# A hybrid attention, pooling, mLSTM and expert layer: finer expert searches, later gating, twelve gate blocks moved into the first pass's branches, and another order of the first loads

## The reference

```
def _layer(x, is_prompt, st, p, rel_bias):
    xn = _rmsnorm(x, p['norm1_g'])
    z = xn @ p['w_in']
    aq, ak, av, pin, cq, ck, cv, ci, cf, co, ga, gb, gc = jnp.split(z, _split_points(), axis=-1)
    ...
    merged = (jax.nn.sigmoid(ga) * (ya @ p['w_br_a']) + jax.nn.sigmoid(gb) * (yb @ p['w_br_b'])
              + jax.nn.sigmoid(gc) * (yc @ p['w_br_c']))
    x = x + merged @ p['w_out']
    x = x + _peer(_rmsnorm(x, p['norm2_g']), ...)

def _peer(x, wq, k1, k2, u, v):     # per block of tokens
    q = (xb @ wq).reshape(blk, PEER_HEADS, 2, PEER_DK // 2)
    s1 = jnp.einsum('thd,kd->thk', q[:, :, 0], k1);  s2 = jnp.einsum('thd,kd->thk', q[:, :, 1], k2)
    v1, i1 = lax.top_k(s1, 16);  v2, i2 = lax.top_k(s2, 16)
    cand = v1[..., :, None] + v2[..., None, :]       # 256 pairs, the best 16 are the experts
    gates = softmax(top_v)
    act = gelu(einsum('td,thkd->thk', xb, u[experts]))
    y = einsum('thk,thkd->td', gates * act, v[experts])
```

## Time and profile before

| | us |
|---|---|
| median of three runs | 3745.59 |
| lowest, highest | 3741.58, 3746.2 |
| the profiled execution | 3749.68 |
| its span in the trace | 3747.9 |
| first gather issued, from the span's start | 395.3 |
| first pass: first matmul of project, branches, merge, output, find | 19.5, 122.3, 193.4, 321.4, 366.2 |
| second pass: the same | 540.2, 712.2, 835.9, 1072.4, 1139.5 |
| third pass: the same | 1335.7, 1527.9, 1659.3, 1895.7, 1963.5 |
| last pass: the same | 2164.2, 2363.5, 2672.1, 2890.0, 2967.1 |

### The profile page before, as it was taken

The page is one execution under the profiler, slowest core; times in us unless marked ns, Lnnn a source line. Parts: engine busy times, 40 slices in busy tenths (PEclk is TensorE's granted clock), DMA queues, the critical chain, the costliest instruction groups (busy, mean ns, idle before and its releaser), DMA issues. The chain is left out here.

```text
span 3747.9 us, 31564 instructions
## 1 busy us (share of the span) xinstructions
PE 3148.9 (84%) x10006; PEld 1809.0 (48%) x10006; DVE 2254.2 (60%) x5201; ACT 1102.6 (29%) x3314; POOL 1174.5 (31%) x1038
## 2 busy tenths in 40 slices
PE   7798879979988889889979799873699898777777
PEld 4587644446665444446655444431466563332222
DVE  1411767674556768865557779872455487764544
ACT  1210333342223333432223324441111233332222
POOL 0000333333333333433323233331233234444442
PEclk9899989989998999999989899986899999999999
DMA  5134889989999999999999899984899699999998
GB/s 168 64 134 158 348 364 387 359 321 365 420 419 361 400 368 414 404 366 391 420 385 392 351 390 402 379 331 175 320 382 397 254 402 404 421 421 421 422 421 356
DMA packets 204912, 1317.39 MB, mean 352 GB/s; under 512 B 23234, under 2 KB 27386, under 8 KB 72097
## 3 DMA queue, kind: packets, MB, share of 16 engines
q0 software_dynamic: 148608, 1082.20, 71.4%
q1 hardware_dynamic: 52681, 220.59, 15.8%
q10 hardware_dynamic: 3456, 12.58, 0.9%
HBM read 1298.97 MB, written 17.64 MB: 351 GB/s over the span
## 5 line engine op out<-in xcount | busy, mean ns | idle before, releaser
L1862 POOL DMA_INDIRECT arena<-uv,eidx x1032 | 1173.9, 1138 | 2544.9 <-PE ps L889 1812.5
L889 PE MATMUL ps<-arena,dgs 128*128 128x512 f32 x3412 | 1638.2, 624 | 310.2 <-ACT dgs L1190 286.4
L1432 DVE CUSTOM_DVE_ANT_0 arena<-arena,xx 128x1024 f32<-128x1024 f32 x1024 | 1232.9, 1222 | 513.1 <-DMA arena<-uv,eidx 488.6
L889 PEld LDWEIGHTS ps<-arena,dgs 128*128 128x128 f32 x3412 | 651.5, 198 | 1122.0 <-issue 669.0
L1171 ACT ACTIVATE gel<-dots 128x2 f32<-128x2 f32 x516 | 104.3, 202 | 1524.7 <-DVE dots L1432 1524.0
L922 PE MATMUL ps<-wbuf,xT 128*128 128x420 f32 (+1 forms) x1152 | 426.1, 519 | 10.2 <-DMA wbuf<-w_z 9.1
L1070 PE MATMUL ps<-xT,wbuf 128*128 128x256 f32 (+1 forms) x1536 | 358.1, 387 | 7.9 <-DMA wbuf<-w_merge 5.8
L1070 PEld LDWEIGHTS ps<-xT,wbuf 128*128 128x128 f32 x1536 | 295.4, 193 | 78.3 <-issue 18.6
L922 PEld LDWEIGHTS ps<-wbuf,xT 128*128 128x128 f32 (+1 forms) x1152 | 204.2, 180 | 232.6 <-issue 220.6
L1190 ACT ACTIVATE dgs<-cst,wgt 128x128 f32<-128x128 f32 x853 | 305.3, 395 | 16.7
L1667 DVE SCALAR_TENSOR_TENSOR T<-T,ps 128x256 f32<-128x256 f32 (+1 forms) x96 | 40.6, 423 | 429.7 <-PE ps L1074 429.7
(11 more groups left out here) (352 smaller groups left out, 1871.5 us busy)
## 6 DMA issues: line engine op xcount, KB each, us to landing
wbuf<-w_merge SPq DMA_DIRECT2D x96, 768.0 KB, 8.5
wbuf<-w_z SPq DMA_DIRECT2D x64, 840.0 KB, 8.7
wbuf<-w_q SPq DMA_DIRECT2D x64, 512.0 KB, 8.1
arena<-uv,eidx POOLq DMA_INDIRECT x1032, 11.6
wbuf<-w_o SPq DMA_DIRECT2D x32, 512.0 KB, 7.4
xin<-x_prompt SPq DMA_DIRECT2D x8, 1024.0 KB, 8.3
grow<-gains SPq DMA_DIRECT2D x8, 512.0 KB, 8.5
xin<-biasfull SPq DMA_DIRECT2D x4, 1024.0 KB, 5.0
```

The lines of the kernel that those rows point to most:

```text
L889: done = mm(ps[:, half, :], dgs[:, j, :], ring[:, j, row_], start=(q == 0), stop=(q == P - 1), skip_group_check=True)
L1432: v.tensor_tensor_reduce(ring[:, j, 0:D], ring[:, j, 0:D], x, 1.0, 0.0, ALU.mult, ALU.add, dots[:, j:j + 1]).then_inc(s["dotted"], 1)
L1862: g.indirect_dma_start(ring[:, j, :], None, uv, bass.IndirectOffsetOnAxis(ap=experts, axis=0)).then_inc(got[j], 16)
```

## The change

It has five parts. The number of slots per stage and `KEPT` stay.

1. **First loads.** SyncE loads x, `cst`, the gains and two `w_z` blocks; the six smaller tables follow (`load_tables`) before the third `w_z` block. The bucket product goes behind the first weight block on TensorE (`buckets`), its copy behind the norm on VectorE. `spread_bias` is issued by ScalarE, behind the copies of the first pair of blocks. TensorE waits for the transposed x of one tile at a time.
2. **Twelve gate blocks.** In the first pass, the gate products of merge units 0 to 11 are computed inside the branches, at five places of each tile (`EARLY_AT`: 1, 2, 1, 1, 0 and 1, 2, 1, 1, 2 blocks), in PSUM banks 0 and 1, and ScalarE copies them to a place that the ring uses later. Two thirds of their `w_merge` blocks are loaded for it, and the last third in the merge.
3. **Later gating.** VectorE's gate of unit k-1 comes between the points of unit k. ScalarE's tanh comes behind the first point of its unit, not ahead of it.
4. **Finer searches.** `topk` has eight places for slots and not four, and in `find` TensorE and ScalarE have a point ahead of each of the two query blocks, and two at the similarities. In `project` each place takes one tile's point.
5. **Slots on VectorE.** `ON_VECTOR` gives it a second place of the eight in `project` (the last pass has four already), a fourth in the last pass's merge, and a fourth in `output`: 197 slots of 1032, and before it was 171. By stage: second pass's project 6 to 12, third pass's 7 to 15, last merge 23 to 31, the three outputs 5, 5, 3 to 6, 6, 5.

The diff, cut to its core:

```diff
+EARLY = 12
+EARLY_AT = ({3: 1, 5: 2, 6: 1, 8: 1, 9: 0}, {3: 1, 5: 2, 6: 1, 8: 1, 9: 2})
...
-    first = [(("f", h, i), 1 if h > 1 else 0) for h in range(PH) for i in range(2)]
-    search = [(("f", h, i), 52 / 16) for h in range(PH) for i in range(2)]
+    first = [(("f", h, i), 1 if h > 1 else 0) for h in range(PH) for i in range(4)]
+    search = [(("f", h, i), 52 / 32) for h in range(PH) for i in range(4)]
...
-ON_VECTOR = {"z": (3,), (LAST, "z"): (1, 3, 5, 7), "b": (1, 5), "m": (1, 4, 6), "o": (1, 3, 5), "f": (2,)}
+ON_VECTOR = {"z": (3, 7), (LAST, "z"): (1, 3, 5, 7), "b": (1, 5), "m": (1, 4, 6), (LAST, "m"): (1, 3, 5, 7), "o": (1, 3, 5, 7), "f": (2,)}
...
+        early = arena[:, NT * ZW + 2048:NT * ZW + 2048 + EARLY * TOK].rearrange("p (u n) -> p u n", u=EARLY)
...
+        def unit(p, i):
+
+            return p * UNITS + i + (EARLY if p or i >= NZ else 0)
...
-            sp.dma_start(cst[:, :], consts[:, 0:C_KEEP]).then_inc(s["setup"], 16)
-            sp.dma_start(T[:, 0:512], consts[:, C_KEEP:C_ALL]).then_inc(s["setup"], 16)
-            sp.dma_start(row[:, :], at(rows, 0, [[0, P], [1, R_ALL]])).then_inc(s["setup"], 16)
-            sp.dma_start(col[:, :], cols).then_inc(s["setup"], 16)
-            sp.dma_start(keys[:, :, :], keysT).then_inc(s["setup"], 16)
-            sp.dma_start(wpool[:, :, :], w_pool).then_inc(s["setup"], 16)
-            sp.wait_ge(s["init_v"], 1)
-            sp.dma_start(T[0:32, 512:520], rel).then_inc(s["setup"], 16)
...
+            sp.dma_start(cst[:, :], consts[:, 0:C_KEEP]).then_inc(s["consts_in"], 16)
+
+            def load_tables():
+
+                sp.wait_ge(s["init_v"], 1)
+                sp.dma_start(T[0:32, 512:520], rel).then_inc(s["setup"], 16)
+                sp.dma_start(T[:, 0:512], consts[:, C_KEEP:C_ALL]).then_inc(s["setup"], 16)
+                sp.dma_start(row[:, :], at(rows, 0, [[0, P], [1, R_ALL]])).then_inc(s["setup"], 16)
+                sp.dma_start(col[:, :], cols).then_inc(s["setup"], 16)
+                sp.dma_start(keys[:, :, :], keysT).then_inc(s["setup"], 16)
+                sp.dma_start(wpool[:, :, :], w_pool).then_inc(s["setup"], 16)
 
...
+            def weights(src, shape, count, sem, base, per, between=(), later=None, part=lambda i: (0, 1)):
...
+                    lo, hi = (int(width * x) for x in part(i))
+                    sp.dma_start(wbuf[:, k, lo:hi], src[i][:, lo:hi]).then_inc(w_in[k], 16)
...
-                weights(w_z, (HALF, ZP), NZ, s["z_mm"], NZ * tiles_before(p), tiles, [lambda: load_bias(p)] if p else [spread_bias], None if p else lambda: load_bias(p))
+                weights(w_z, (HALF, ZP), NZ, s["z_mm"], NZ * tiles_before(p), tiles, [lambda: load_bias(p)] if p else [load_tables], None if p else lambda: load_bias(p))
+                if p == 0:
+                    weights(w_merge, (12, P), EARLY, s["gate_mm"], 0, 1, part=lambda i: (0, 2 / 3))
...
+                        part=lambda i: (2 / 3 if p == 0 and i < EARLY else 0, 1))
...
+                if which:
+                    pe.wait_ge(s["xT_ready"], norms(p, which, len(tiles_of(p))))
...
+                        if c == 0:
+                            pe.wait_ge(s["xT_ready"], norms(p, 0, i + 1))
...
+                    if p == c == 0:
+                        buckets()
+
+            gates_done = [0]
+
+            def gates_early(units):
+
+                for u in range(gates_done[0], gates_done[0] + units):
+                    pe.wait_ge(w_in[u % 2], 16 * ((NZ + u) // 2 + 1))
+                    if u >= 2:
+                        pe.wait_ge(s["early_out"], u - 1)
+                    wv = wbuf[:, u % 2, 0:KC * P].rearrange("p (c n) -> p c n", c=KC)
+                    for c in range(KC):
+                        last = mm(ps[:, u % 2, 0:TOK], wv[:, c, :], xT[:, c, 0:TOK], start=(c == 0), stop=(c == KC - 1))
+                    last.then_inc(s["gate_mm"], 1)
+                gates_done[0] += units
 
...
+                    if p == 0:
+                        gates_early(EARLY_AT[t][3])
...
-                    for c in range(KC):
-                        last = mm(ps[:, 2 + 2 * b, m], wv[:, c, :], xT[:, c, m], start=(c == 0), stop=(c == KC - 1))
-                    last.then_inc(s["gate_mm"], 1)
+                    if p or k >= EARLY:
+                        for c in range(KC):
+                            last = mm(ps[:, 2 + 2 * b, m], wv[:, c, :], xT[:, c, m], start=(c == 0), stop=(c == KC - 1))
+                        last.then_inc(s["gate_mm"], 1)
...
+                    for k in range(2):
+                        point(p, "f", h, k)
+                        if h + 1 < PH:
+                            queries(h + 1, [k])
+                    point(p, "f", h, 2)
                     if h + 1 < PH:
                         similarities(h + 1)
+                    point(p, "f", h, 3)
...
+            def spread_bias():
+
+                act.wait_ge(s["buck_sb"], 1)
+                table = T[0:AH, 1024:1408]
+                act.dma_start(bass.AP(tensor=biasfull.tensor, offset=0, ap=[[2 * P, AH], [AH * 2 * P, P], [1, 2 * P]]),
+                              bass.AP(tensor=table.tensor, offset=table.offset + P - 1, ap=[table.ap[0], [-1, P], [1, 2 * P]])
+                              ).then_inc(s["scratch_w"], 16)
+
...
+                    if p == 0 and c == 1:
+                        spread_bias()
...
+            def gates_early(units):
+                for u in range(gates_kept[0], gates_kept[0] + units):
+                    act.wait_ge(s["gate_mm"], u + 1)
+                    f(early[:, u, :], ps[:, u % 2, 0:TOK], ACT.Copy).then_inc(s["early_out"], 1)
+                gates_kept[0] += units
...
-                    act.wait_ge(s["gate_mm"], 3 * KC * p + k + 1)
+                    point(p, "m", k, 0)
                     act.wait_ge(s["merged"], KC * p + k // 3 + 1)
-                    f(sgs[:, b, m], ps[:, 2 + 2 * b, m], ACT.Tanh, scale=0.5).then_inc(s["sig_done"], 1)
-                    point(p, "m", k, 0)
+                    if p == 0 and k < EARLY:
+                        act.wait_ge(s["early_out"], k + 1)
+                        f(sgs[:, b, m], early[:, k, :], ACT.Tanh, scale=0.5).then_inc(s["sig_done"], 1)
+                    else:
+                        act.wait_ge(s["gate_mm"], 3 * KC * p + k + 1)
+                        f(sgs[:, b, m], ps[:, 2 + 2 * b, m], ACT.Tanh, scale=0.5).then_inc(s["sig_done"], 1)
...
-                for k in range(3 * KC):
+
+                def gate(k):
                     b = k % 3
                     n = 3 * KC * p + k
-                    point(p, "m", k, 0)
                     dve.wait_ge(s["sig_done"], n + 1)
...
+                for k in range(3 * KC):
+                    point(p, "m", k, 0)
+                    if k:
+                        gate(k - 1)
                     point(p, "m", k, 1)
+                gate(3 * KC - 1)
...
+                between(0)
                 for k, t in pairs:
                     last = v.max_index(ii[:, k, t, 0:8], vv[:, k, t, 0:8], side_in[0:rows_, k, t, :])
                 last.then_inc(s["idx1"], 1)
-                if between:
-                    between(0)
+                between(1)
...
+                    search(p - 1, h, lambda i: at(4 * (h - SOON[p - 1]) + i // 2, i % 2))
...
-                    search(p, h, lambda i: point(p, "f", 2 * h + i // 2, i % 2))
+                    search(p, h, lambda i: point(p, "f", 2 * h + i // 4, i % 4))
...
```

119 lines of the change are left out of this document (66 added, 53 removed).

## The result

The changed kernel takes 3684.32 us (median of 4, 3682.12 to 3687.32) where the kernel before took 3745.89 beside it (median of 4): a ratio of 0.9835, 95% interval 0.9818 to 0.9852. That is 62 us less. The profiled execution took 3687.3 us (span 3685.5). The forecast was 3685. The total is met, and the sum behind it is not: the first pass gave half of what was forecast, the later passes half as much again. The rest of this document is about these two errors, which cancel; that they do is luck.

The account below looks back on a forecast made before the run. From 395 us on gather DMA bounds the kernel (377 GB/s against 420, 343 us shortfall); before, the first pass's own work. 3749.7 - 11.6 (opening) - 17 (gates) - 32 (later passes) = 3689.1, as median 3685 us; range 3655 to 3720.

Parts of the forecast that it names:

- Opening: First pass up to its branches: earlier norm and projection start and no weight-block wait save 11.6 us, bounds 2 and 14.
- With 4.5 us it is there; I take the whole 8.3: First projection: the fourth weight block, issued about 28, lands before 33.4 us, so TensorE's whole 8.29 us wait goes.
- Rival (3): First projection: the spread still delays a weight block, the fourth stalls, 10 us come back, 3695 us; chance 0.08.
- Twelve gates: First pass: gate blocks moved into branches cost 16 us there and save 33 in the merge, 17 us net.
- The walk through one tile: First pass's branches: five gate blocks of 17.25 us, partly filling TensorE's waits, make the first tile end 7 us later.
- Slots on VectorE: Later passes: moved slots save 7 us in the second projection, 1 in the third, 8 in last merge, 2 in outputs.
- Later gating: Merges of later passes: VectorE's gate after the next unit's dots saves 3 us in each of two merges.
- Finer searches: Find stages: eight points per search instead of four save 2.5 us in each of three, 0.5 in the first.
- (1) *Only the first pass pays: Later passes: already full where it matters, earlier freed slots only wait in the queue; 3717 us, chance 0.17.
- (5) *A slot on VectorE holds the ring longer: Later passes: 26 moved slots make GpSimd wait longer for VectorE, 95 us against 29 gained; 3811 us, chance 0.04.
- (4): First pass's branches: gates cost all of their 41.4 us and later passes give nothing; 3742 us, no change; chance 0.03.
- (2) *Nearly all: Later passes: they give nearly all they have, 65 us; 3652 us, chance 0.13.

Follow-up runs that it names:

- the three placings of the runs: Bias spread issued by ScalarE at 27.96 us (changed kernel, 0.9835), by SyncE at the same moment (0.9864), or by ScalarE near 9.5 us (0.9826).
- the run with that entry alone: Changed kernel without only the last merge's entry in VectorE's slot table (slots 1, 4, 6 of eight there, not 1, 3, 5, 7): ratio 0.9836 to the kernel before.

## Why the prediction was right, and where it was not

**Opening: forecast 11.6 us, measured -0.2.** The step that failed is "With 4.5 us it is there; I take the whole 8.3". The first half of the term held (start 14.33 instead of 13.8, bucket product with its copy 22.01 - 20.39 = 1.6 instead of 2.3 us). The prediction then followed the fourth block, issued at 28 and needed at 33.4, found it in time, and it was. It did not follow the fifth, issued at 33.6 with the spread in full course. With a spread of some 22 us and a load every 5.7, at least one load falls under it, wherever it stands; the three placings of the runs stall 12.21, 15.83 and 10.93 us. Loads that were issued while it ran took 10 to 18 us in the kernel before and in the changed one, where they take 4.5 alone. The row that said so stood in the earlier trace rows (a load of 13.9 us); I put it down to the place in the queue. Rival (3) is what happened, at a chance of 0.08, with 12.2 us for its 10, and on the next block. By the Trainium skill, DMA: Bandwidth & Descriptors, section Issuing engines are not separate DMA queues, a second issuer saves only the time of issuing, so the move to ScalarE's queue gives next to nothing; the runs agree to within 3.6 us (12.21 against 15.83). The same page, in the section Why a DMA increments its semaphore by 16 and not by 1, says that a DMA runs on the largest number of engines, 16 at most, that divides the slowest dimension of both of its sides, which is 8 here; the four or five tenths of the DMA view agree with it, and so do the 53.6% of the spread from DRAM. The 1.4 us for the half clock didn't come either, since a wait was still there: the clock was 0.50, its lower level of 1.2 GHz, from 46 to 52 us, and TensorE had been idle since 39.2:

```profile
46.00:52.00 6.00, 0.59 (x1) 0.50 (x2) 0.00 (x0) 0.00 (x0) 0.00 (x0) 0.50 0.49 163
```

**Twelve gates: forecast 17 us net, measured 12.8.** The walk through one tile held: the traces show the first block at 130.93, intra at 143.80, the transposes of P at 149.42, the last block at 152.50 and the product of P and V at 156.05, within 0.2 of the times of the walk. Only the whole tile grew by 5.4 us (37.5 instead of 32.1) and not by 7, since the products of P and V run at full clock too. That the branches cost 16.1 us against the run without early gates, where the forecast says 16, is in part luck: 3.4 us of clock came back there without any gate. What was mis-sized is the merge: 30.2 us less, and 1.3 more in the output, instead of 33 less; by the other runs' first merges it is 29 to 34 less, so this error is small and not clear of the noise. The twelve short units, with the wait for the first full block behind them, take 237.82 - 206.32 = 31.5 us instead of 29 (the pairs begin 4.6 to 5.5 us apart, and the last of them 7.1 before the full block), and the first full gate block meets the half clock, 0.53 from 237.8 to 244:

```profile
211.17 3.72 PE L1114 MATMUL ps<-yT,wbuf 128*128 128x256 f32 x16 [1.13 <-DMA wbuf<-w_merge]
215.80 3.74 PE L1114 MATMUL ps<-yT,wbuf 128*128 128x256 f32 x16 [0.91 <-DMA wbuf<-w_merge]
...
237.82 6.59 PE L1110 MATMUL ps<-xT,wbuf 128*128 128x256 f32 x16 [3.38 <-DMA wbuf<-w_merge]
```

16 matmuls take 6.59 us there, and 3.62 at full clock: 3 us that the sum did not have. (The lower bound of -8 us was taken from 33 - 41.4; with the term's own lower bound of 31 it is -10.)

**First gather: forecast 366 us, 380.50.** The prediction named anything beyond 375 as its own refutation, and it was one, for the first pass.

**Slots on VectorE: forecast 18 us, measured 13.** The second projection gave 10.2 for 7, the last merge 5 to 7 for 8, but by the run with that entry alone the 6 do not reach the end.

**Later gating: forecast 6 us, measured 19.** The failing step is "3 us in each of two merges". For these two it was right (3.2 and 2.7 us). The third merge, the last one, was left out, and there it is 14 us. The argument for the small number was that TensorE frees five of eight slots at fixed points. That held in all three merges of the kernel before, and still the gating alone takes 15 us off the last one, where GpSimd's wait for VectorE's rows fell from 82.3 to 3.3 us. The place of the gate was priced by whom VectorE waits for, and not by what GpSimd waits for at VectorE; that wait, 225.8 us in all, stood in the earlier trace rows.

**Finer searches: forecast 8 us, measured 9, for the wrong reason.** 11 to 15 us came from the norm stretches, which had no term. The find stages of the first three passes, which had all of it, changed by 2 us or less between fine and coarse. The last find stage cost 7 to 8 us by its length and 11 by the ratios, and no bound of the prediction reached there.

**The sum.** Opening 11.8 too much and gates 4 too much, against 13 too little for the gating, 1 for the searches, and 5 too much for the slots: on these terms 7 us too much, where the total was right to 1 us; the terms that rest on two ratios are open by some 9 us each, so the 7 can't be placed. The range 3655 to 3720 held the time because errors of both signs met in it, which is luck. The prediction's own points of failure, above all the first gather, judge it better than its total.

**Rivals.** (1) *Only the first pass pays* fell, with 47.6 us from the later passes. (5) *A slot on VectorE holds the ring longer* fell with GpSimd's 112.9 us for VectorE's rows, where the rival asked for more than 225.8. (4) fell with the run without early gates. (2) *Nearly all* asked for 65 us of the later passes and the forecast for 32; the 47.6 lie half way.

## What to carry to other kernels

A long DMA of small pieces can stall the double-buffered loads that are issued while it runs, on another queue as well as on its own: follow the loads up to the end of the long one, not only the next one, and try it in parts that fit between two loads. Price an edit in every stage that it touches, the last one too; the gating was priced for two merges, and the third gave 14 of its 19 us. A finer interleaving pays at the points where an engine waits with landed work in hand, and it cost time in the one stage where TensorE was busy 0.95 of the time: try it stage by stage, not for all of them.

## What the runs showed of the hardware that I had not expected

The same 1024 pieces of 1 KB to DRAM took 0.114 us each in one DMA out of SBUF, 0.047 in eight DMAs of 128, and 0.047 in one DMA from DRAM to DRAM. With the one DMA out of SBUF the engines were busy four or five tenths of the time and moved 46 to 49 GB/s, and a weight load of 840 KB took 17.8 us (33.6 to 51.4) on another queue, where it takes 4.5 alone. Placed 17 us earlier it still stalled TensorE for 10.93 us instead of 12.21; in eight parts it stalled it not at all, and out of DRAM, at 182 pieces a us instead of 47, for 0.89 us.
